# Tokens sorted by class in a two-layer hybrid decoder trunk, with norms last in a DVE tick and one set of probabilities turned by DVE

## What is computed

```python
for i in range(2):
    h = rmsnorm(x, norm[i])
    x = x + (fox_attention(h) if i == 0 else dilated_attention(h, positions))
    x = x + square(relu(rmsnorm(x, mlp_norm[i]) @ w1[i])) @ w2[i]

# dilated_attention: three groups g, each with its own q, k, v (16 heads of 64)
q, k = partial_rope(rmsnorm(q_g), positions), partial_rope(rmsnorm(k_g), positions)
# window 128 dilation 1, window 512 dilation 4, window 2048 dilation 16:
# a token looks at itself and at tokens of its residue class (mod dilation) in the window
o_g, lse_g = softmax_attention(q, k, v_g, mask_g)
o = sum over g of softmax(lse)_g * o_g;   return o @ w_out
```

## Time and profile before

| | |
|---|---|
| median of 3 runs | 1610.9 us (1609.99 to 1611.69) |
| profiled execution | 1607.93 us, its span 1605.9 us |
| TensorE matmul busy | 1560.0 us (97%) |
| DVE busy | 927.3 us (58%) |
| ACT busy | 708.7 us (44%) |
| POOL busy | 447.0 us (28%) |

### The profile page before, as it was taken

One profiled execution on the slowest core, in us unless ns is written; L12 is line 12 of the kernel. 1 busy time (PEld: TensorE's weight loads), 2 busy tenths in 40 slices (PEclk: granted clock), 3 DMA queues, 4 the chain that ended last, 5 costly groups with the idle time before them and its releaser, 6 DMA issues.

```text
span 1605.9 us, 23589 instructions
## 1 busy us (share of the span) xinstructions
PE 1560.0 (97%) x8706; PEld 1297.2 (81%) x8706; DVE 927.3 (58%) x1572; ACT 708.7 (44%) x1188; POOL 447.0 (28%) x608
## 2 busy tenths in 40 slices
PE   7999999999999999899999999999998999999998
PEld 6776666888888887799988888998766888888886
DVE  4456544557474748544647576554644456565748
ACT  5433344354444545434434334433443353535453
POOL 3412200021011721262527365443822110101110
PEclk9999999999999999999999999999999999999999
DMA  6221110467565754432222422222232377475753
GB/s 174 80 66 41 46 48 14 144 141 177 131 179 131 181 133 79 131 92 79 67 80 66 133 56 64 79 74 60 66 120 93 119 161 205 105 203 110 190 124 79
DMA packets 111354, 173.48 MB, mean 108 GB/s; under 512 B 13216, under 2 KB 45984, under 8 KB 111008
## 3 DMA queue, kind: packets, MB, share of 16 engines
q1 hardware_dynamic: 91664, 134.51, 27.0%
q0 software_dynamic: 17408, 33.56, 12.9%
q10 hardware_dynamic: 2192, 4.20, 0.8%
HBM read 165.89 MB, written 6.36 MB: 107 GB/s over the span
## 4 chain that ended last, share of the span: by engine, by line
PE 80%; DVE 8%; POOL 5%; ACT 3%; issue 3%; DMA 1%; ACTq 0%; DVEq 0%; POOLq 0%
PE ps L567 53%; PE ps L841 15%; PE ps L627 3%; PE ps L659 3%; PE ps L641 2%; POOL qrs L1663 2%; PE ps L671 2%; DVE w_l L1472 1%; PE ps L598 1%; POOL qss L1662 1%; ACT w_h L917 1%; ACT p_sb L984 1%; DVE qss L1249 1%; DMA raw<-in_mlp_w 1%; DVE e_all L1518 1%
## 5 line engine op out<-in xcount | busy, mean ns | idle before, releaser
L567 PE MATMUL ps<-w_h,act_h 128*128 128x512 f32 x768 | 317.9, 414 | 8.9 <-issue 3.6
L567 PE MATMUL ps<-w_h,act_l 128*128 128x512 f32 x768 | 307.7, 401 | 0.0
L567 PE MATMUL ps<-w_l,act_h 128*128 128x512 f32 x768 | 306.6, 399 | 0.0
L567 PEld LDWEIGHTS ps<-w_h,act_h 128*128 128x128 f32 x768 | 192.5, 251 | 28.4 <-issue 11.7
L567 PEld LDWEIGHTS ps<-w_l,act_h 128*128 128x128 f32 x768 | 192.4, 251 | 16.0
L567 PEld LDWEIGHTS ps<-w_h,act_l 128*128 128x128 f32 x768 | 193.1, 251 | 14.3
L567 PE MATMUL ps<-act_h,w_h 128*128 128x512 f32 x512 | 200.0, 391 | 0.6 <-DVE w_l L1443 0.6
L567 PE MATMUL ps<-act_h,w_l 128*128 128x512 f32 x512 | 199.5, 390 | 0.0
L567 PE MATMUL ps<-act_l,w_h 128*128 128x512 f32 x512 | 199.5, 390 | 0.0
L984 ACT ACTIVATE p_sb<-ps,negmax 128x128 f32<-128x128 f32 (+3 forms) x256 | 93.3, 427 | 239.0 <-DVE negmax L1297 179.9
L841 PE MATMUL ps<-w_h,op_h 128*128 128x512 f32 x448 | 176.0, 393 | 0.0
(11 more groups left out here) (198 smaller groups left out, 2599.3 us busy)
## 6 DMA issues: line engine op xcount, KB each, us to landing
w_raw<-in_dil_w_in SPq DMA_DIRECT2D x72, 512.0 KB, 3.8
raw<-in_mlp_w SPq DMA_DIRECT2D x64, 512.0 KB, 4.8
raw<-in_mlp_w POOLq DMA_DIRECT2D x48, 512.0 KB, 5.8
w_raw<-in_mlp_w SPq DMA_DIRECT2D x32, 512.0 KB, 4.9
w_raw<-in_fox_w_in SPq DMA_DIRECT2D x22, 512.0 KB, 3.6
p_sb<-in_mlp_w SPq DMA_DIRECT2D x16, 512.0 KB, 5.2
pT_sb<-in_mlp_w SPq DMA_DIRECT2D x16, 512.0 KB, 6.1
w_raw<-in_mlp_w POOLq DMA_DIRECT2D x16, 512.0 KB, 6.8
```

Of the source, the lines that this page charges most:

```text
L567: return mm(ps_out, lhs[i], rhs[j], start=(k == 0 and term == 0), stop=(k == KT - 1 and term == 2))
```

## The change

Three things are changed.

- Tokens sorted by class. The host hands in x so that each block of 128 tokens is sorted by residue class mod 16, and puts the rows of the result back. `prepare(3, ...)` writes the activations so that the four tiles of x interleave (every fourth column); a bank of sets 2, 3, 5, 6 and the q and k banks of 4 and 7 then take 128 neighbouring columns, only the value banks of 4 and 7 take every fourth. The q and k of dilation 1 are put back into the order of x by `qk_evacuate`. Positions are held in one order, masks are made in sorted order by small TensorE products and copied by DVE, and `reorder` swaps its two patterns.
- Norms. DVE adds the epsilon behind its own sum of squares; POOL only raises to the power. In a DVE tick `norm_qk` comes after `output`.
- Probabilities of dilation 16 (sets 3 and 6). Sorted, a class of 32 tokens is a diagonal block of 32x32, so `turn_probs` is dropped on TensorE and `probs_back` is a DVE transpose from SBUF to SBUF.

The core of the diff:

```diff
+def turned_by_pe(s):
+    return SETS[s][0] != 2
...
+        block_rows = rest[:, 0:P // 2].bitcast(BF16)
+        by_time = rest[:, P // 2:3 * P // 2].bitcast(BF16)
...
-        def tok(act, k, tile, layout):
-            if layout == 0:
+        def tok(act, k, tile, every_fourth):
+            if not every_fourth:
                 return act[:, k, tile * P:(tile + 1) * P]
-            return act[:, k, :].rearrange("p (i r) -> p r i", r=NT)[:, tile, :]
+            return act[:, k, :].rearrange("p (m t) -> p t m", t=NT)[:, tile, :]
...
         def prep_dst(n, half, t):
             i = (slice(None), slice(4 * half, 4 * half + 4), slice(t * P, (t + 1) * P))
+            if n == 3:
+                c = slice(4 * half, 4 * half + 4)
+                return [x[:, c, :].rearrange("p k (m t) -> p t k m", t=NT)[:, t, :, :] for x in (act_h, act_l)]
...
-                sp.dma_start(acc_dram.rearrange("(p r) c -> p r c", r=NT), acc12[:, :, :, :].rearrange("p r h c -> p r (h c)")).then_inc(acc_out, 16)
+                sp.dma_start(acc_dram.rearrange("(r p) c -> p r c", r=NT), acc12[:, :, :, :].rearrange("p r h c -> p r (h c)")).then_inc(acc_out, 16)
...
-                               acc_dram.rearrange("(t p) c -> p t c", p=P)).then_inc(acc_in, 16)
+                               acc_dram.rearrange("(p t) c -> p t c", p=P)).then_inc(acc_in, 16)
...
             def turn_probs(s, a):
+                if not turned_by_pe(s):
+                    return
...
+                            mm(ps_s[1][:, 0:2 * P], block_rows, by_time, start=True, stop=True)
                             mm(ps_s[0][:, 0:NT], spread, place[:, :], start=True, stop=True).then_inc(turned_full, 1)
-                        last = token_bank(B, k, term, b % 4, 0 if kind == "fox" else LAYOUT[kind])
+                        last = token_bank(B, k, term, b % 4, kind == 0 and b >= QK_SET)
...
+                    pe.wait_ge(pool_done, 1)
+                    mm(ps_s[1][:, 0:3 * P], class_rows[:, :], class_masks[:, :, :].rearrange("p n k -> p (n k)"), start=True, stop=True).then_inc(masks_full, 1)
...
-                dst = (qT if b < 4 else kT)[s % 2][:, :, (b % 4) * P:(b % 4 + 1) * P]
-                fn(dst, ps_q[:, :].rearrange("p (i t) -> p i t", i=4), ACT.Copy, scale=hg[:, g:g + 1]).then_inc(qt_done, 1)
+                dst, src = (qT if b < 4 else kT)[s % 2], ps_q[:, :].rearrange("p (i t) -> p i t", i=4)
+                if kind == 0:
+                    dst = dst[:, :, :].rearrange("p i (t r m) -> p r i t m", t=NT, r=NT)[:, b % 4, :, :, :]
+                    src = src.rearrange("p i (m t) -> p i t m", t=NT)
...
             def norm_turned():
                 dve.wait_ge(turned_full, 1)
+                v.tensor_copy(causal[:, :], ps_s[1][:, 0:P])
+                v.tensor_copy(residue[:, :], ps_s[1][:, P:2 * P])
...
-                    v.tensor_reduce(qss[:, n % 2, :], sq[:, :].rearrange("p (h d) -> p h d", d=HD), AX, ALU.add).then_inc(qss_done, 1)
+                    if b == 0 and s in (0, 2):
+                        dve.wait_ge(aux_done, 1 + s // 2)
+                    link(v.tensor_reduce(qss[:, n % 2, :], sq[:, :].rearrange("p (h d) -> p h d", d=HD), AX, ALU.add))
+                    v.tensor_scalar(qss[:, n % 2, :], qss[:, n % 2, :], xaux[:, norm_slot(s), b % 4:b % 4 + 1], None,
+                                    ALU.add).then_inc(qss_done, 1)
...
             def probs_back(s, a):
-                dve.wait_ge(pt_full, a + 1)
+                if not turned_by_pe(s):
+                    dve.wait_ge(exp_done, a + 1)
+                    dve.wait_ge(pv_done, a - 1)
+                    v.transpose(pT_sb[:, a % 2, :], p_sb[:, a % 2, :]).then_inc(pt_done, 1)
+                    return
+                dve.wait_ge(pt_full, turned_count(a))
...
                         if a < nt:
                             maxima(attend, t0 + a)
-                        if proj is not None and a > 0:
-                            for s, b in banks_of_tick(proj, attend, a - 1):
-                                norm_qk(s, b)
...
                         if 3 <= a <= nt + 2:
                             output(attend, t0 + a - 3)
+                        if proj is not None and a > 0:
+                            for s, b in banks_of_tick(proj, attend, a - 1):
+                                norm_qk(s, b)
...
+                    dve.wait_ge(masks_full, 1)
+                    v.tensor_copy(causal[:, :], ps_s[1][:, 0:P])
+                    v.tensor_copy(banded[:, 0:P], ps_s[1][:, P:2 * P])
+                    v.tensor_copy(banded[:, P:2 * P], ps_s[1][:, 0:P])
+                    v.tensor_copy(upto_t[:, :], ps_s[1][:, 2 * P:3 * P]).then_inc(masks_done, 1)
...
                 pool.wait_ge(qss_done, n + 1)
-                link(g.tensor_scalar(qss[:, n % 2, :], qss[:, n % 2, :], xaux[:, norm_slot(s), b % 4:b % 4 + 1], None, ALU.add))
                 g.tensor_tensor(qrs[:, n % 2, :], qss[:, n % 2, :], m_half[:, :], ALU.pow).then_inc(qrs_done, 1)
```

More of the change, by code:

```diff
@@ L54 @@
 WR = 8
[L55 removed]
+NC = 4
+BY_CLASS = "p (r c j) -> p r c j"
+BY_BLOCK = "p (c j t) -> p c j t"
 SETS = [("fox", 0), ("fox", 1), (1, 0), (2, 0), (0, 0), (1, 1), (2, 1), (0, 1)]
@@ L204, in out_fill, with set_of, turned_count @@
     return range(3 * i, 3 * i + 3) if 0 <= i < NT else range(0)
+def turned_by_pe(s):
+    return SETS[s][0] != 2
+def set_of(a):
+    return max(s for s in range(len(SETS)) if TICK0[s] <= a)
+def turned_count(a):
+    return sum(turned_by_pe(set_of(b)) for b in range(a + 1))
 def out_early(a):
@@ L251, in trunk @@
                 ones_t = sb("ones_t", [P, P], F32, first)
+                class_rows = sb("class_rows", [P, P], BF16, first)
+                class_masks = sb("class_masks", [P, 3, P], BF16, first)
                 b_f = sb("b_f", [P, NH], F32, first)
@@ L298, in trunk @@
         tab_b = sb("tab_b", [P, 6, NT, ROT])
-        pos_i = sb("pos_i", [P, 2, NT], I32)
-        pos_f = sb("pos_f", [P, 2 * NT])
+        pos_i = sb("pos_i", [P, NT], I32)
+        pos_f = sb("pos_f", [P, NT])
         freq = sb("freq", [P, HALF])
-        ang = sb("ang", [P, 2 * NT, HALF])
-        turns = sb("turns", [P, 2 * NT, HALF])
-        sin_t = sb("sin_t", [P, 2 * NT, HALF])
+        ang = sb("ang", [P, NT, HALF])
+        turns = sb("turns", [P, NT, HALF])
+        sin_t = sb("sin_t", [P, NT, HALF])
         sinh_t = turns
@@ L434, in mlp_unit, with norm_slot @@
             return i * PER_CHUNK + (BANK_MLP[layer] + p)
-        def norm_slot(s):
+        def norm_slot(s, value=False):
             kind = SETS[s][0]
-            return 0 if kind == "fox" else 2 if LAYOUT[kind] == 0 else 4
+            return 0 if kind == "fox" else 2 if kind == 0 and value else 4
         def wait_bank_free(pe, B):
@@ L572, in weights_ready, with token_bank @@
                     pe.wait_ge(wl_done, more + (B + k // 2 + 1))
-            def token_bank(B, k, term, tile, layout=0, out=False):
+            def token_bank(B, k, term, tile, every_fourth=False, out=False):
                 slot = (B // 4 * 4 + k // 2) % WR
@@ L766, in terms @@
                     for m in range(first, end):
-                        last = token_bank(B0 + b, m // 3, m % 3, b % NT, 0, True)
+                        last = token_bank(B0 + b, m // 3, m % 3, b % NT, False, True)
                     if end == 3 * KT:
@@ L945, in qk_evacuate @@
                 g = (0 if kind == "fox" else 2 + 2 * kind) + b // 4
-                dst = (qT if b < 4 else kT)[s % 2][:, :, (b % 4) * P:(b % 4 + 1) * P]
-                fn(dst, ps_q[:, :].rearrange("p (i t) -> p i t", i=4), ACT.Copy, scale=hg[:, g:g + 1]).then_inc(qt_done, 1)
+                dst, src = (qT if b < 4 else kT)[s % 2], ps_q[:, :].rearrange("p (i t) -> p i t", i=4)
+                if kind == 0:
+                    dst = dst[:, :, :].rearrange("p i (t r m) -> p r i t m", t=NT, r=NT)[:, b % 4, :, :, :]
+                    src = src.rearrange("p i (m t) -> p i t m", t=NT)
+                else:
+                    dst = dst[:, :, (b % 4) * P:(b % 4 + 1) * P]
+                fn(dst, src, ACT.Copy, scale=hg[:, g:g + 1]).then_inc(qt_done, 1)
             def bank_event(s, b, attend):
@@ L978, in probs @@
                 act.wait_ge(max_done, a + 1)
-                if a >= 2:
-                    act.wait_ge(pt_full, a - 1)
+                if a >= 2 and turned_by_pe(set_of(a - 2)):
+                    act.wait_ge(pt_full, turned_count(a - 2))
+                elif a >= 2:
+                    act.wait_ge(pt_done, a - 1)
                 col = 0
@@ L1287, in maxima @@
                     if kind == 0 and segs[0][2] == 1:
-                        v.tensor_tensor(ps_s[a % 2][:, 0:P], ps_s[a % 2][:, 0:P], causal[:, :], ALU.add)
+                        v.tensor_tensor(ps_s[a % 2][:, 0:P], ps_s[a % 2][:, 0:P], banded[:, P:2 * P], ALU.add)
                         col = P
@@ L1610, in _ @@
             out_projection(BANK_FOX_OUT, 1)
```

(15 more changed lines are left out.)

75 lines of the change are left out of this document (38 added, 37 removed).

## The result

The changed kernel takes 1598.7 us (1597.4 to 1598.9) where the kernel before takes 1610.5 beside it: ratio 0.9927, 95% interval 0.9911 to 0.9943, or 11.8 us less. I had forecast 24.2 less. The direction is right, the size is not: half of the gain is missing. The time lies at the high end of my range (1577 to 1600).

A forecast was written before the change was run, and what follows sets the result against it. TensorE was taken to bound most dilated steps, a loop through ACT, DVE and POOL 7|6. Terms -11.0 + 0.5 - 4.6 - 4.4 - 1.2 - 1.0 - 2.5 gave -24.2 us from 1610.9: 1586.7 us, range 1577 to 1600.

The forecast's parts named there:

- Turned by DVE: 4|3 and 7|6: DVE's turn takes the copy's 0.68 us, four TensorE transposes a tick go; -2.5 us.
- rival 1: 4|3 and 7|6: DVE becomes the bound, its turn taking 1.42 us instead of 0.68; 1595.8 us, chance 0.18.
- Norms last: DVE ticks: norm multiplication after the output; -4.6 us in 7|6, -4.4 in 1|0, -1.2 in 5|4, -1.0 in 2|-.
- the loop of 6.86: 7|6: loop through ACT and DVE falls from 7.44 us to 6.86, 0.58 in each of 8 ticks, -4.6 us.
- The add: Sums of squares: add moves from POOL to DVE, 0.25 us there, 64 times; POOL's chain loses 0.75.
- Rival 2: 7|6 and 4|3: POOL holds up DVE's added operation; loop 7.32 us, kernel 1592.2 us, chance 0.10.
- 4|3: Step projecting set 4 while set 3 is attended: TensorE never idle, so its work counts; forecast -1.4 us.
- Tokens by class: Dilated steps: 48 banks become contiguous, 8 value banks take every fourth token; -11.0 us.
- The store: After the first MLP: 8 preparations write every fourth place on ACT and DVE; +0.5 us, up to +3.8.
- rival 3: After the first MLP: strided stores cost 0.48 us each; kernel 1590.0 us, chance 0.08.
- -|7: Last step, attending set 7, with output: +1.1 us forecast, though the text put its two strided banks where PE waits.
- 1|0, 5|4: Steps projecting set 1 while attending 0, and 5 while attending 4: TensorE waits less; -4.4 and -4.5 us.

The follow-up runs named there:

- the late turn: The changed kernel with VectorE's transpose of the widest dilation moved one tick ahead in VectorE's order, into its idle time; 1591.5 us, ratio 0.9882.
- the late merge: The kernel with the late turn, with GpSimd's three merge operations of a tick moved between its power and the rotation; ratio 0.9901.
- the version that beats both: The kernel with the late turn, the split of weights before the sum, and merges behind the power only in 4|3 and 7|6; 1584.3 us, ratio 0.9849.

## Why the prediction was wrong

**Turned by DVE: the step that failed first.** The duration was right (0.70 against 0.68). What failed is "taken as no change", which looked at the length of the operation and not at what it holds. TensorE's turn freed the exponentials' buffer; in the change VectorE's transpose does, and it stands behind the maxima of a later tick. That put it into the round: 7.87 in the first rounds of 4|3, in which nothing is merged yet, against 7.19 with the late turn. My rival 1 had VectorE as the bound through a slow transpose; the mechanism was another, a wait in a fast one.

**Norms last: the loop of 6.86.** I replaced the start of the chain by 4.80 and kept its closing at the merge factors (2.06). With the power gone, the round closes through the exponentials instead: from the sum's start to theirs 3.64 and on to the next sum 3.55, 7.19 in the kernel with the late merge. That link was already to be seen in the earlier trace rows: the maxima end at 870.59, 3.35 after the sum's start; with ScalarE's 3.55 and 0.25 for the add that is 7.15, beside the 7.44 of the earlier trace rows. So some 0.3 a round was to be had, not 0.58, and I multiplied it by 8: of the seven distances from square to square in 7|6 five are rounds of this loop before and three after.

**The add.** Rival 2 is the case too, with 0.56 to 0.60 in after for 0.23, 0.35 to 0.44 a round, in the rounds with merges. Together: 6.86, and 0.33 for the exponentials' link, 0.68 for the turn, 0.35 for the add make 8.22. The Trainium skill, SBUF — State Buffer, section Who interferes with whom, states that VectorE operations with two SBUF inputs block against GpSimd operations that read SBUF, and scalar ones in a two-port mode against any, while sums do not. The traces agree, though none shows the mode: split 1.41 to 1.7 or 2.09, subtraction 0.16 to 0.54, add 0.23 to 0.68, the sums always 0.67 to 0.69; and the add that reads PSUM stays at 0.23.

**4|3.** Forecast -1.4, measured +4.36. I took it to be TensorE's (7.23 a tick on average without the turns). At 8.22 it is not. The late rotation (7.5 us in all at L700) is a consequence: with VectorE's work unchanged and the loop cut, it is 3.4 in the version that beats both. With the late turn and the late merge 4|3 and 7|6 take 83.24 and 72.72, where the forecast had 82.4 and 73.2: so the wait behind the turn and GpSimd's hold-up are what it lacked. The round is 7.19 there and not 6.86: 7|6 gets to its number also through the rounds outside the loop.

**Tokens by class.** Right in 3|2 and 6|5, to 0.15 us each. In 2|- I had 1.5 too much, and most of it lies in the first bank. From the second bank on the step falls from 69.9 to 66.3, 3.6 where its share of the forecast was 4.0. The first bank grows from 8.4 to 9.2, and TensorE waits 0.6 there for `act_l`, which the strided store writes. The kernels with the same instructions in this step take 73.1 to 75.2, and all of that lies in the first bank too: 7.9 with the granted clock at full, 9.2 to 9.5 with 3.4 us at half, 10.0 with 5.5 to 6.2.

**The store.** Mis-sized: 0.40 on VectorE and 0.60 on ScalarE for 512 elements, so rival 3's 0.48 was the better price and the row I chose, a strided read, the worse witness. But of the 8 us that the eight such stores cost on the two engines only some 2 are exposed: 1.3 at the end of the MLP, and 0.7 in 2|- (75.18 in the kernel whose add reads PSUM, 74.49 without the strided store, with the granted clock at half for 5.5 us in both). The rest lies beside TensorE's work. The Trainium skill's rule that the prediction set against this part (SBUF — State Buffer, Specifications) has the sign right: a store at every fourth place is dearer on both engines.

**-|7.** The 1.1 in the table is the share of set 7's four strided value banks; two of them run in 7|6 and two here. The prediction's sum charges all four, though its text has these two where PE waits anyway. They cost 0.7 to 0.8 (99.0 to 99.1 in the kernels where the clock holds, 98.3 with neighbouring tokens). The rest is 0.8, with the granted clock at 0.52 for 3.5 us (1.2 instead of 2.4 GHz). TensorE waits 2.0 for an output just before, but so it does in the late turn, without the fall. The fall is not the change's own: the profile of the kernel before with neighbouring tokens shows it in this step too.

**1|0, 5|4.** Right within 0.3 and 0.7, both partly by luck. The clock's fall in 1|0 did go. But with the add left on GpSimd the two steps take 105.24 and 96.38, 4.9 and 5.4 less than before, more than I gave them (4.4 and 4.5); the moved add, which I had counted as a gain, takes 0.8 and 1.6 of it back.

## What to carry to other kernels

When an operation changes its engine, list what it releases as well as what it reads: every buffer that it frees gets the new engine's queue position as its price, however short the operation. Before a wait is credited with its whole length, work out the next-longest loop through the same two engines; only the difference is to be had, and only in as many rounds as close that loop. And where VectorE and GpSimd both work on SBUF, shifting one short operation only moves the hold-up to its neighbour; order them so that VectorE works on PSUM meanwhile, and look step by step, since the order that gained 2.2 us in 7|6 cost 3.6 in 5|4.
